# A feed-forward stage's end with three down rounds in place of four, the last round's tile 0 ahead of tile 1's gate and up products

## What is computed

```python
D_MODEL, SEQ, D_FF = 1024, 256, 2816

def swiglu_ffn(x, w_gu, w_down):
    a, u = jnp.split(x @ w_gu, 2, axis=-1)
    return (jax.nn.silu(a) * u) @ w_down

for l in range(2):
    x = layer_norm(ALPHA * x + 0.5 * swiglu_ffn(x, ffn1_w_gu[l], ffn1_w_down[l]), ln1_g[l], ln1_b[l])
    x = layer_norm(ALPHA * x + hybrid_mixer(x, ...), ln2_g[l], ln2_b[l])
    x = layer_norm(ALPHA * x + 0.5 * swiglu_ffn(x, ffn2_w_gu[l], ffn2_w_down[l]), ln3_g[l], ln3_b[l])
```

## Time and profile before

| | |
|---|---|
| median of three runs | 1372.7 us |
| profiled execution: time, and span in the trace | 1372.61 us, 1370.8 us |
| TensorE matmuls, share of the span | 98% |
| VectorE, ScalarE, GpSimd | 72%, 48%, 8% |
| DMA, mean over the span | 194 GB/s, 265.41 MB |
| mean granted TensorE clock | 0.996 |

### The profile page before, as it was taken

One profiled execution on the slowest core, in us unless ns is written; L12 is line 12 of the kernel. 1 busy time (PEld: TensorE's weight loads), 2 busy tenths in 40 slices (PEclk: granted clock), 3 DMA queues, 4 the chain that ended last, 5 costly groups with the idle time before them and its releaser, 6 DMA issues.

```text
span 1370.8 us, 18393 instructions
## 1 busy us (share of the span) xinstructions
PE 1339.5 (98%) x7084; PEld 1136.4 (83%) x7084; DVE 990.0 (72%) x1548; ACT 652.4 (48%) x1019; POOL 104.0 (8%) x153
## 2 busy tenths in 40 slices
PE   8999999999999999999999999999999999999997
PEld 7888888888888887888888878888888997799976
DVE  5676677887677676766677795686775688965877
ACT  5444345624444444444437444354355666456652
POOL 0111000011011001111010010111100000000000
PEclk9999999999999999999999999999999999999999
DMA  7977755338776557677464357777476433474430
GB/s 249 325 228 229 237 180 184 129 102 257 231 229 218 195 183 254 217 230 243 162 209 160 120 163 255 245 247 230 156 255 211 147 124 124 138 236 149 142 123 32
DMA packets 174855, 265.41 MB, mean 194 GB/s; under 512 B 16496, under 2 KB 131312, under 8 KB 174256
## 3 DMA queue, kind: packets, MB, share of 16 engines
q1 hardware_dynamic: 163056, 223.63, 49.8%
q0 software_dynamic: 11712, 40.60, 9.2%
HBM read 263.13 MB, written 1.07 MB: 193 GB/s over the span
## 4 chain that ended last, share of the span: by engine, by line
PE 81%; DVE 12%; DMA 4%; ACT 2%; issue 1%; SPq 1%; DVEq 0%
PE ps L748 24%; PE ps L750 24%; PE ps L749 24%; DVE w_lo L1206 5%; PE ps L817 4%; DMA w_raw<-in_w_in 2%; PE ps L991 2%; PE ps L961 1%; DMA w_raw<-in_ffn_w_gu 1%; DVE small L1236 1%; DVE y L1235 1%; PE ps L1017 1%; PE ps L862 1%; ACT w_hi L1047 1%; DVE col_lo L1218 1%
## 5 line engine op out<-in xcount | busy, mean ns | idle before, releaser
L1206 DVE TENSOR_TENSOR w_lo<-w_raw,w_hi 128x1024 fp32r<-128x1024 f32 (+3 forms) x424 | 494.3, 1205 | 184.3 <-ACT w_hi L1047 183.2
L1047 ACT ACTIVATE w_hi<-w_raw 128x1024 fp32r<-128x1024 f32 (+3 forms) x424 | 422.0, 1041 | 311.8 <-DMA w_raw<-in_ffn_w_gu 173.3
L748 PE MATMUL ps<-w_hi,col_hi 128*128 128x512 f32 (+2 forms) x1216 | 477.9, 393 | 10.8 <-DVE col_lo L1218 5.5
L750 PE MATMUL ps<-w_hi,col_lo 128*128 128x512 f32 (+2 forms) x1216 | 466.5, 384 | 0.0
L749 PE MATMUL ps<-w_lo,col_hi 128*128 128x512 f32 (+2 forms) x1216 | 465.7, 383 | 0.0
L748 PEld LDWEIGHTS ps<-w_hi,col_hi 128*128 128x128 f32 x1216 | 228.8, 188 | 58.1 <-DVE w_lo L1206 11.1
L750 PEld LDWEIGHTS ps<-w_hi,col_lo 128*128 128x128 f32 x1216 | 228.5, 188 | 45.3
L749 PEld LDWEIGHTS ps<-w_lo,col_hi 128*128 128x128 f32 x1216 | 229.0, 188 | 40.8
L748 PE MATMUL ps<-w_hi,lat_hi 128*128 128x512 f32 (+2 forms) x416 | 158.0, 380 | 0.0
L750 PE MATMUL ps<-w_hi,lat_lo 128*128 128x512 f32 (+2 forms) x416 | 156.5, 376 | 0.0
L749 PE MATMUL ps<-w_lo,lat_hi 128*128 128x512 f32 (+2 forms) x416 | 156.5, 376 | 0.0
(11 more groups left out here) (137 smaller groups left out, 1168.1 us busy)
## 6 DMA issues: line engine op xcount, KB each, us to landing
w_raw<-in_ffn_w_gu SPq DMA_DIRECT2D x172, 512.0 KB, 5.1
w_raw<-in_w_in SPq DMA_DIRECT2D x54, 1024.0 KB, 5.2
w_raw<-in_ffn_w_down SPq DMA_DIRECT2D x44, 1024.0 KB, 5.2
mod<-in_w_ada POOLq DMA_DIRECT2D x32, 768.0 KB, 7.9
w_raw<-in_w_out SPq DMA_DIRECT2D x16, 1024.0 KB, 5.0
norm_g<-in_ln_g POOLq DMA_DIRECT2D x8, 512.0 KB, 4.9
norm_b<-in_ln_b POOLq DMA_DIRECT2D x8, 512.0 KB, 6.3
w_raw<-in_w_uq SPq DMA_DIRECT2D x4, 864.0 KB, 4.9
```

Source lines behind the costliest of these rows:

```text
L748: pe.matmul(dst, a_hi, b_hi, start=start, stop=False)
L750: return pe.matmul(dst, a_lo, b_hi, start=False, stop=stop)
L1047: act.activation(half_of(w_hi[j], n, h), half_of(raw[j], n, h), ACT.Copy).then_inc(hi_ready, 1)
L1206: tt(half_of(w_lo[j], n, h), half_of(raw[j], n, h), half_of(w_hi[j], n, h).bitcast(F32), ALU.subtract)\
```

## The change

It sets `TAIL` to 3, which no code uses any more, and writes the end of `ffn_jobs` out. Down round 7 moves into round 9, so that rounds 8, 9 and 10 are left. In the last round the gate and up products of tile 0 are followed by `ht` of round 9, down 8 of tile 0, the transposes of round 10 for tile 0 alone, down 9 and 10 of tile 0 and its norm. Then come the gate and up products of tile 1, down 8, the transposes of round 10 for tile 1, down 9, the next stage's `xt`, down 10 and norm of tile 1. The `ht` of round 10 becomes two jobs of two transposes each, with a tile number as fourth entry; ACT and DVE copy half as many columns in each.

```diff
--- before.py
+++ after.py
@@ -29,7 +29,7 @@
 F = 2816
 FU = 256
 ROUNDS = F // FU
-TAIL = 4
+TAIL = 3
 UNIT = KT * FU
 HALF = 512
 ALPHA = (2 * DEPTH) ** 0.25
@@ -156,9 +156,8 @@
             jobs += [("spread", s, r - 3), ("modrow", s, r - 3)]
         if r < 2 + MOD_STEPS:
             jobs += [("modsum", s, r - 2)]
-        jobs += gu(r, 1)
-        if lag < ROUNDS - TAIL:
-            jobs += down(lag, 0) + down(lag, 1)
+        if r < ROUNDS - 1:
+            jobs += gu(r, 1) + down(lag, 0) + down(lag, 1)
             lag += 1
         if r == 4 and s == FIRST2 - 1:
             jobs += [("modload", FIRST2)]
@@ -166,12 +165,9 @@
             jobs += [("fold", FIRST2)]
     if s == FIRST2 - 1:
         jobs += [("gains", FIRST2)]
-    tail = list(range(ROUNDS - TAIL, ROUNDS))
-    jobs += down(tail[0], 0) + down(tail[1], 0) + [("ht", s, ROUNDS - 1)] + down(tail[2], 0) + down(tail[3], 0)
-    jobs += [("norm", s, 0)]
-    for r in tail[:-1]:
-        jobs += down(r, 1)
-    return jobs + [("xt", s + 1, 0)] + down(tail[-1], 1) + [("norm", s, 1)]
+    end = ROUNDS - 1
+    jobs += down(end - 2, 0) + [("ht", s, end, 0)] + down(end - 1, 0) + down(end, 0) + [("norm", s, 0)] + gu(end, 1)
+    return jobs + down(end - 2, 1) + [("ht", s, end, 1)] + down(end - 1, 1) + [("xt", s + 1, 0)] + down(end, 1) + [("norm", s, 1)]
 
 
 def row(s, name, i):
@@ -852,9 +848,9 @@
                     b = gu_bank(s, r, i)
                     rows_by(n, j, (s, r, i), i, bank(b), col_hi, col_lo, range(4 * h, 4 * h + 4), slice(0, 512), h == 0, h == 1)
                 elif kind == "ht":
-                    r = job[2]
-                    pe.wait_ge(hidden_done, at["hidden", (s, r, 1)])
-                    turn(job, 0, [(hidden[:, r % 2, i, f * P:(f + 1) * P], f * S + i * P) for f in range(2) for i in range(TT)])
+                    r, tiles = job[2], job[3:] or range(TT)
+                    pe.wait_ge(hidden_done, at["hidden", (s, r, tiles[-1])])
+                    turn(job, 0, [(hidden[:, r % 2, i, f * P:(f + 1) * P], f * S + i * P) for f in range(2) for i in tiles])
                 elif kind == "spread":
                     b, m = TURN[job][0]
                     pe.wait_ge(mod_summed, at["modsum", ("modsum", s, job[2])])
@@ -862,7 +858,7 @@
                     pe.matmul(bank(7, MOD_W), ones[:, :], ada_sum, start=True, stop=True).then_inc(turned[b], 1)
                 elif kind == "down":
                     r, i = job[2:]
-                    turns_done(("ht", s, r))
+                    turns_done(("ht", s, r, i) if r == ROUNDS - 1 else ("ht", s, r))
                     q = 2 * (r % 4)
                     wide(n, j, s, ("down", r), i, lat_hi, lat_lo, (q, q + 1), r == 0, r == ROUNDS - 1)
                 elif kind == "T":
@@ -1092,8 +1088,13 @@
                 elif kind == "ht":
                     q = 2 * (job[2] % 4)
                     b = turn_wait(job)
-                    act.activation(lat_hi[:, q:q + 2, :].rearrange("p a b -> p (a b)"), bank(6 + b), ACT.Copy)\
-                        .then_inc(hi_part, 1)
+                    if len(job) > 3:
+                        toks = slice(job[3] * P, (job[3] + 1) * P)
+                        act.activation(lat_hi[:, q:q + 2, toks], bank(6 + b).rearrange("p (f s) -> p f s", f=2)[:, :, toks],
+                                       ACT.Copy).then_inc(hi_part, 1)
+                    else:
+                        act.activation(lat_hi[:, q:q + 2, :].rearrange("p a b -> p (a b)"), bank(6 + b), ACT.Copy)\
+                            .then_inc(hi_part, 1)
                 elif kind == "T":
                     name = (job[2], job[3])
                     b, first, tiles = TURNED[name]
@@ -1302,8 +1303,13 @@
                 elif kind == "ht":
                     q = 2 * (job[2] % 4)
                     b = TURN[job][0][0]
-                    lo_part(job, bank(6 + b), lat_hi[:, q:q + 2, :].rearrange("p a b -> p (a b)"),
-                            lat_lo[:, q:q + 2, :].rearrange("p a b -> p (a b)"), b)
+                    if len(job) > 3:
+                        toks = slice(job[3] * P, (job[3] + 1) * P)
+                        lo_part(job, bank(6 + b).rearrange("p (f s) -> p f s", f=2)[:, :, toks], lat_hi[:, q:q + 2, toks],
+                                lat_lo[:, q:q + 2, toks], b)
+                    else:
+                        lo_part(job, bank(6 + b), lat_hi[:, q:q + 2, :].rearrange("p a b -> p (a b)"),
+                                lat_lo[:, q:q + 2, :].rearrange("p a b -> p (a b)"), b)
                 elif kind == "modsum":
                     if at["modsum", job] == 1:
                         dve.wait_ge(c_ready, 1)
```

## The result

Nine runs of the changed kernel gave a median of 1375.41 us (1374.88 to 1379.25), nine of the kernel before on the same chip 1371.5 (1369.26 to 1373.46). The ratio is 1.0036, 95% interval 1.0028 to 1.0044: 3.9 us slower, where +4.3 was forecast. The profiled execution took 1375.33, its span is 1373.5.

The account below looks back on a forecast made before the run. TensorE, busy in 98% of the span, was taken as the bound. A chain 0.9 us late at four stage ends (3.6) plus 0.7 for `KV` loads gives 4.3 on 1372.7: 1377.0 us, own range 1375.3 to 1379.0.

Parts of the forecast that it names:

- The first wait: At round 10's transposes for tile 0, TensorE waits 1.02 us for VectorE's low part of round 9.
- The second wait: At the next stage's tile 0 transposes, 0.8 us for VectorE's low part of round 10; costs nothing on top.
- Which sum decides: At the four stage ends: VectorE's chain, 3.6 us in all, not TensorE's new waits of 7.7 against old 7.6.
- the chain on VectorE: From landing of the next stage's second unit through its split to tile 1's norm: 0.9 us late per stage end.
- how late N1 is: Next stage's second weight unit (N1): its load is requested 0.85 us later than in the kernel before.
- N1's own landing: Load of the next stage's second weight unit: taken as landing 5.08 us after its request, as before.
- rival (b): Burst of loads 2.72 us apart at each stage end: 0.6 us more each, 2.4 on top, 1379.4; chance 0.12.
- the KV term: Ends of stages 0 and 3, where the next stage's first unit is `KV`: later landing adds 2 x 0.35 us.
- rival (c): Idle spots at next-stage transposes lower TensorE's clock at two of four stage ends: 3.2 on top, 1380.2; chance 0.08.
- Norm 1: Norm of tile 1 at the stage end: ends 0.9 to 1.3 us later than before.
- rival (d): Head start of tile 0's norm moves the whole stage end, the 7.6 us of waits go: about 1366; chance 0.04.

Follow-up runs that it names:

- experiment 1: Changed kernel with the split of down 10 moved behind the transposes of round 9; 1369.45 us, ratio to the kernel before 0.9997.
- experiment 4: Kernel before with round 10's transposes as two entries, one directly behind the other, nothing else; 1375.08 us, ratio 1.0032.
- experiment 2: Changed kernel with the split of the next stage's first unit moved behind round 10's second transposes; 1375.43 us, ratio 1.0036.
- experiment 3: Changed kernel with both splits moved behind, down 10's and that of the next stage's first unit; 1370.35 us, ratio 1.0005.
- experiment 5: Kernel before with round 10's transposes as two entries and down 9 of tile 0 between them; 1370.82 us, ratio 1.0000.
- experiment 6: Changed kernel with the split of down 9 also put ahead of the transposes of round 9; 1391.9 us, ratio 1.0153.
- experiment 7: Kernel before with only down 7 moved ahead, three down rounds left, round 10's transposes one entry; 1374.42 us, ratio 1.0033.
- experiment 8: Kernel before with down 7 moved ahead and stage 6's two gain loads issued behind the norm of tile 0; 1370.37 us, ratio 1.0000.
- experiment 9: Kernel before with down 7 moved ahead and the next stage's second unit split behind the norm of tile 0; 1367.8 us, ratio 0.9974.

## Why the prediction was right, and which terms were off

**The first wait** was forecast at 1.02 us, by the copy of the pattern in the earlier trace rows. The trace shows 1.00, 1.00, 0.99 and 0.99 us of idle time. What it costs is a little more, see below. Experiments 1 and 4 show that this wait carries the loss: without it the time is that of before, and a wait of the same size in the same place of the old order costs as much.

**The second wait** was forecast at 0.8 for a landing of 5.1 us, growing with it. N0 landed in 5.5 and the wait was 1.14: 0.34 more for 0.4 more. The other stages had 1.16, 0.99 and 0.71. It costs nothing on top, as said (experiments 1 and 2).

**Which sum decides** was the step most open to doubt: TensorE's new waits against its old ones give about nothing, the chain on VectorE gives 0.9 a seam. Experiment 2 decides for the chain, and so does the seam length, which follows N1's landing to 0.01 us. The forecast that the next stage's first matmul waits for nothing held in all four seams.

**Mis-sized: how late N1 is.** Counted from round 9's `spread`, its request came at 31.80 or 31.81 before and at 32.76 after in all four seams: 0.95 late, not 0.85. That `ht10` is half as long ahead of that point was to save 0.17, and did (experiment 1, without the wait: 31.58 to 31.60, which is 0.2 earlier than before). It is the wait that was put too low: it delays the request by 1.17. `lat_lo` ended 4.52 us after the transposes of `ht9` began (177.02 to 181.54), as forecast (4.53), but `ht10,0` started only at 181.69. These 0.15 are not in the forecast's 4.53 - 3.51. The 1.00 of the trace hides them, since idle time is counted from the end of the last matmul, 0.39 long, behind which the next would have started after 0.23.

**Mis-sized: N1's own landing.** The prediction kept it at that of before. It rose by 0.43 in stage 0 (5.08 to 5.51), 0.55 in stage 2 (where the unit comes as two loads), 0.18 in stage 3 and 0.12 in stage 5. Request and landing together give +1.38, +1.51, +1.14 and +1.07, against +1.39, +1.50, +1.14 and +1.06 of the seams: of the 5.1, the late request is 3.8 and the slower landing 1.3. The latter is a small form of rival (b): N0 is now in flight when N1 is asked for. N1 took 5.1 to 5.6 in experiments 1 to 3 too, where that is so, and 5.0 to 5.3 in before and in experiment 5, where it is not; but in experiment 4, where it is not either, it took 5.1 to 5.4, so this cause is likely and not shown. The window 195 to 200 shows 388 GB/s and a share of 1.04, as before. Why stages 0 and 2 lose more than 3 and 5 is not shown.

**Right size, wrong place: the KV term.** 2 x 0.35 stood for `KV` landing later than another N0. It did land in 5.5 and 5.4, against 5.1 in stages 2 and 5. But the two seams with the extra loss are 0 and 2, and not 0 and 3. The extra goes with N1's landing; `KV`'s own lateness only lengthens the second wait, which costs nothing. So the 0.7 in the sum had the wrong cause. That it stood in for part of another loss was luck.

**The clock**, rival (c), did not come in, though `xt` with its wait made a stretch of about 2 us without a large matmul. The Trainium skill's warning on idle arrays, "TensorE: Matmul & The Clock Gate", section "What's actually happening", is borne out by experiments 6 and 7, at 3.27 and 4.51 us; behind the change's own waits, 1.2 us and less, the clock stayed at 1.00.

**Norm 1** was to end 0.9 to 1.3 later; in stage 0, counted from the seam's start, it ended 1.39 later. In the sum of rival (d), 1372.7 less 7.6 is 1365.1 and not 1366, which changes nothing here.

**The total.** The seams give 5.1 where 4.3 was forecast, the medians 3.9: the mechanism was right, and both the wait and the landing were put too low, so that the forecast lies this near to the medians is partly luck. That the predicted 1377.0 lies above the measured 1375.4 is mostly the starting point: before measured 1371.5 in nine runs, 1.2 less than the median of three. What stays open is the 1.2 us between the seams' sum and the medians; a difference between two single traces can't settle it.

## What to carry to other kernels

Where engines work through one list in order, a moved job also moves what a planner hangs on due times: work out by hand where each split lands, and which small result on a shared bank then stands behind it. A wait costs its full length if it lies ahead of the request of the load that the next chain begins with, and little or nothing if it lies behind it and takes the place of a wait that was there. To see which load that is, subtract each unit's landing from the seam's end in every seam: where the rest is the same to a hundredth, the chain begins. Let the norm go ahead of a split that a late load can hold, and keep loads of another queue away from the one load that is waited for.

## What the runs showed of the hardware

- **The clock after a wait.** At waits of 3.27 and 4.51 us TensorE's clock was at 1.2 GHz, the lower of its two levels, for some 3.5 to 7 us, of which a part can lie within the wait. At shorter waits the outcome differed. These are the lines of the same wait of stage 6 in after, before and experiment 8:

```profile
1042.44 0.39 PE L744 MATMUL ps<-col_hi,w_hi 128*128 128x256 f32 x1 [1.85 <-DVE w_lo L1207]
```

```profile
1038.26 0.39 PE L748 MATMUL ps<-col_hi,w_hi 128*128 128x256 f32 x1 [2.12 <-DVE w_lo L1206]
```

```profile
1035.67 0.39 PE L748 MATMUL ps<-col_hi,w_hi 128*128 128x256 f32 x1 [2.45 <-DVE w_lo L1206]
```

  Behind 1.85 the clock stayed at 1.00, behind 2.12 it was 0.54 over 3.4 us, and behind 2.45 it was 0.66 over 5.0 us. So a wait that grows by a few tenths can cost more than it grows by. There is one case of each, so whether the length of the wait or something else decided between them is not shown.
- **Two queues at once.** N1's load of 1 MB took 9.7 us in stage 5 of experiment 7 (and 9.8 in experiment 9) beside 512 KB from POOL's queue, against 5.4 and 5.9 in stages 0 and 3 of experiment 7, and 5.7 with POOL's loads moved. In the last three microseconds (988 to 991) the DMA engines were busy for a share of 0.31, at 116 GB/s, so the tail of the load kept about a third of them at work. Why it is so uneven was not tried.
